# Three orders changed in a two-block transformer kernel: the loads of a norm's rows, the context rows, and the row maxima of a neighbourhood attention

## What is computed

```python
for l in range(2):
    h = layer_norm(a * h + hybrid_mixer(h, ...), ln1_g[l], ln1_b[l])
    h = layer_norm(a * h + cross_attention(h, mem, ...), ln2_g[l], ln2_b[l])
    h = layer_norm(a * h + swiglu(h, ffn_wi[l], ffn_wo[l]), ln3_g[l], ln3_b[l])

sh_a, sc_a, g_a, sh_f, sc_f, g_f = adaln(c, w_ada, b_ada)
hc = rms(ctx) * (1 + csc_a) + csh_a               # the context rows
q, k, v, u, vs = project(rms(h) * (1 + sc_a) + sh_a)
kc, vc = project_kv(hc)
s_win = q @ k_win * scale + bias                  # 8 heads of 64, 256 rows
s = concatenate([s_win, q @ kc * scale])
o_na = softmax(s) @ [v_win, vc]
o_sg = gelu(u) * (w_s @ layernorm(gelu(vs)) + b_s)
x = h + g_a * (concatenate([rms(o_na), rms(o_sg)]) * out_gain) @ w_out
x = x + g_f * hier_moe(rms(x) * (1 + sc_f) + sh_f)
```

## Time and profile before

| | |
|---|---|
| runs | 1566.18, 1569.23, 1570.77 us |
| median | 1569.23 us |
| profiled execution | 1569.23 us |
| its span | 1567.3 us |
| mean granted TensorE clock | 0.993 |
| PE busy | 1536.3 us (98%) |
| DVE busy | 1167.5 us (74%) |
| ACT busy | 920.0 us (59%) |

### The profile page before, as it was taken

How to read it: one execution, slowest core, us unless ns; L and a number is a source line. 1 busy time by engine, 2 the same in 40 slices (tenths; PEclk the granted TensorE clock), 3 DMA queues, 4 the chain that set the end, 5 groups by cost and what they waited for, 6 DMA issues and landing times.

```text
span 1567.3 us, 20279 instructions
## 1 busy us (share of the span) xinstructions
PE 1536.3 (98%) x8024; PEld 1288.4 (82%) x8024; DVE 1167.5 (74%) x1628; ACT 920.0 (59%) x1421; POOL 82.2 (5%) x75
## 2 busy tenths in 40 slices
PE   9999999999999999999999999999999989999997
PEld 9988898888888799889888887888867778878785
DVE  7448866667885683688566679877676789999998
ACT  6468644655444444775447554544355468888884
POOL 0010000001000000100000000000200000000005
PEclk9999999999999999999999999999899999999999
DMA  7535335437775354553354458884441349999994
GB/s 288 208 123 218 135 116 215 161 135 260 256 271 210 134 211 161 188 188 133 137 215 165 158 216 322 335 320 149 165 151 54 113 152 378 365 377 374 369 368 166
DMA packets 52201, 339.35 MB, mean 217 GB/s; under 512 B 7835, under 2 KB 8477, under 8 KB 13316
## 3 DMA queue, kind: packets, MB, share of 16 engines
q1 hardware_dynamic: 48932, 331.79, 56.9%
q0 software_dynamic: 3168, 6.20, 1.1%
HBM read 332.82 MB, written 10.49 MB: 219 GB/s over the span
## 4 chain that ended last, share of the span: by engine, by line
PE 89%; DVE 6%; ACT 2%; issue 1%; DMA 1%; POOL 1%; SPq 0%; DVEq 0%; ACTq 0%; POOLq 0%
PE bank L843 26%; PE bank L845 25%; PE bank L844 25%; PE bank L849 5%; DVE wls L2255 2%; PE bank L1002 2%; PE bank L1130 1%; DMA raw<-in_ws_dram 1%; PE bank L1191 1%; PE bank L1169 1%; PE bank L1110 1%; PE bank L1390 1%; POOL sm L3214 1%; ACT whs L1611 1%; DVE arena L2234 0%
## 5 line engine op out<-in xcount | busy, mean ns | idle before, releaser
L2255 DVE TENSOR_TENSOR wls<-raw,whs 128x1024 fp32r<-128x1024 f32 x426 | 507.0, 1226 | 164.6 <-ACT whs L1611 163.8
L1611 ACT ACTIVATE whs<-raw 128x1024 fp32r<-128x1024 f32 x426 | 429.4, 1052 | 209.9 <-PE bank L845 166.6
L843 PE MATMUL bank<-whs,P1h 128*128 128x512 f32 (+1 forms) x732 | 290.5, 397 | 2.1 <-issue 2.1
L845 PE MATMUL bank<-whs,P1l 128*128 128x512 f32 (+1 forms) x732 | 284.5, 389 | 0.0
L844 PE MATMUL bank<-wls,P1h 128*128 128x512 f32 (+1 forms) x732 | 283.7, 388 | 0.0
L843 PE MATMUL bank<-whs,P0h 128*128 128x512 f32 (+1 forms) x640 | 256.0, 400 | 1.3 <-DVE P0l L2225 1.2
L845 PE MATMUL bank<-whs,P0l 128*128 128x512 f32 (+1 forms) x640 | 248.9, 389 | 0.0
L844 PE MATMUL bank<-wls,P0h 128*128 128x512 f32 (+1 forms) x640 | 248.3, 388 | 0.0
L843 PEld LDWEIGHTS bank<-whs,P1h 128*128 128x128 f32 x732 | 137.6, 188 | 29.4 <-issue 3.0
L845 PEld LDWEIGHTS bank<-whs,P1l 128*128 128x128 f32 x732 | 137.4, 188 | 29.0
L844 PEld LDWEIGHTS bank<-wls,P1h 128*128 128x128 f32 x732 | 137.8, 188 | 26.6
(11 more groups left out here) (300 smaller groups left out, 2511.2 us busy)
## 6 DMA issues: line engine op xcount, KB each, us to landing
raw<-in_ws_dram SPq DMA_DIRECT2D x264, 1024.0 KB, 4.9
landing<-in_ws_dram SPq DMA_DIRECT2D x38, 1024.0 KB, 7.0
lnb<-in_ln_g_dram SPq DMA_DIRECT2D x6, 512.0 KB, 5.8
lnb<-in_ln_b_dram SPq DMA_DIRECT2D x6, 512.0 KB, 7.1
ydram<-arena POOLq DMA_DIRECT2D x4, 512.0 KB, 8.5
mid<-in_bias_dram SPq DMA_DIRECT2D x1, 2048.0 KB, 9.5
h<-in_x_dram SPq DMA_DIRECT2D x2, 512.0 KB, 3.7
lnb<-in_mem_dram SPq DMA_DIRECT2D x1, 1024.0 KB, 13.1
```

The source lines that it names most:

```text
L843: e.matmul(out, x[0], w[0], start=start, stop=False, skip_group_check=skip)
L845: return e.matmul(out, x[1], w[0], start=False, stop=stop, skip_group_check=skip)
L1611: e.activation(hi, src, ACT.Copy, bias=0.0, scale=1.0).then_inc(*high.done(n, f))
L2255: e.tensor_tensor(lo, src, f32(hi), ALU.subtract).then_inc(*low.done(n, f))
```

## The change

Three edits. The number for the rows of the second norm is taken at the end of `cq_w` and no longer in `co_w`, so that two weight units that were issued ahead of these rows now stand behind them. The pauses of the context rows are cut from 12 ticks to 4 on PE, ACT and DVE, so that the squares are ACT's at the first tick of the feed-forward, `ctxeps` and `cn` are DVE's at the second to fourth, and the four parts of `ctx_columns` fall at the `between` ticks of chunks 1 to 4, which were those of chunks 3 to 6. And DVE does the row maximum of item i at step i for each item, which it did for two items at every even step. PE's and ACT's orders in the attention stay.

```diff
@@ PE, cross @@
                 mm.here("cq_end", l)
+                issued["n", l, 2] = W.dma
...
                 def loose():
                     W.loose = True
                     W.feed(2)
-                    issued["n", l, 2] = W.dma
@@ PE, after cross(1) @@
                     mm.here("late")
-                    W.side.append(iter([None] * 12))
+                    W.side.append(iter([None] * 4))
@@ ACT @@
                     def ctx_rows():
-                        for _ in range(8):
-                            yield
                         for t in range(2):
                             ac.wait_ge(landed["ctx"])
                             wait_for(at_all("late"))
@@ DVE @@
                     def ctx_rows():
-                        for _ in range(9):
-                            yield
+                        yield
                         for t in range(2):
                             ve.wait_ge(act, "ctxsq", t)
@@ DVE, attention2 @@
                     if i >= 5:
                         weigh2(i - 5)
-                    if i < n and i % 2 == 0:
+                    if i < n:
                         scores2(i)
-                        scores2(i + 1)
                     for f, *at in beside.get(i, ()):
```

## The result

After the change the kernel takes 1579.25 us (median of 4 runs, 1578.11 to 1580.88), before it 1569.09 (4 runs, 1566.18 to 1570.77). The ratio is 1.0061, with a 95% interval of 1.0047 to 1.0075: slower by 9.6 us by the ratio, 7.4 to 11.8 by its interval. The forecast was 1577.0 us. The profiled execution of the changed kernel took 1578.79 us, 1576.9 of them span, 9.6 more than that of before. In 24 further runs on record the changed kernel has a median of 1577.2 us, and the kernel before has 1569.7 in the 56 runs that the experiments are compared with; so 9.6 us may be somewhat high. Lines of helpers have moved by two in it: DVE's L2253 is L2255 of before.

The account below looks back on a forecast made before the run. PE, with an instruction in it for 98% of the span, was taken as the bound, so only its waits and clock count. The edits' 0 + 2.95 + 4.85 = 7.8 us on 1569.2 gave 1577.0 us, range 1569 to 1582.

Parts of the forecast that it names:

- Edit 1, 0: SP's load queue: two weight units behind the norm's row loads still land in time; cost 0.
- Edit 2, the third quarter, 2.75 us: Layer 1's feed-forward: PE waits 2.75 us for unit 145's low half, held up behind ACT's squares.
- Edit 2, the sixth quarter, 1.0 us: Layer 1's feed-forward: PE waits 0.6 and 0.4 us for unit 146's two low halves.
- the prediction's last line: Wrong if squares start before 893, PE's second pair does not wait, or the clock falls in either stretch.
- rival (c): Clock falls where waits grow; 3 us per 10 us stretch, one or two more giving 1580 to 1583 us; chance 0.12.
- Edit 2, the wait at 948, -0.8 us: Layer 1's feed-forward: less DVE lateness shortens PE's wait for a low part; gain 0.8 us, bounds 0 and 1.9.
- Edit 3, 4.85 us: Attention: PE's score pairs wait for late bank reads, 2.0, 1.0, 0.4, 0.95 us, plus small terms; 4.85 us, bounds 0 and 8.
- The sum: Whole kernel: 0 + 2.95 + 4.85 = 7.8 us slower, 1577.0 us.
- (a): Only one of the two stretches, feed-forward or attention, waits: 1573.3 or 1572.2 us; chance 0.22.
- (b): Not slower: DVE's relief at 948 is the whole effect, 1567.3 us, if squares start before about 892; chance 0.10.
- (d): SP's queue edit shows: a unit late by its whole landing costs 4.9 us, 1582 us with the rest; chance 0.02.

Follow-up runs that it names:

- ctx_single: Kernel before with only the context rows' change, one square ahead of unit 145's splits, the other and all behind it as in ctx_behind; 1571.00 us, ratio 1.0012.
- ctx_triple: Kernel before with only the context rows' change, three squares ahead of unit 145's splits (that of t=0 taken twice); 1576.24 us, ratio 1.0045.
- ctx_behind: Kernel before with the context rows early (7 ticks, not 4), the squares behind ACT's splits of units 145 and 146; 1569.90 us, ratio 0.9999.
- rows_only: Kernel before with only the second norm's row number taken at the end of cq_w; 1570.49 us, ratio 0.9999.
- maxima_only: Kernel before with only DVE's row maximum done one item a step; 1573.91 us, ratio 1.0024.
- read_pair: Kernel before with DVE reading both banks at the even step, the odd item's maximum only at the odd step; 1570.86 us, ratio 1.0012.
- single_both: Kernel before with DVE's maximum one item a step and PE also issuing one item's scores a step; 1580.39 us, ratio 1.0070.
- ctx_only: Kernel before with only the context rows' pauses cut from 12 ticks to 4; 1574.42 us, ratio 1.0035.

## Why the prediction was right, point by point

**Edit 1, 0.** Right: 0.9999.

**Edit 2, the third quarter, 2.75 us.** Right in place, in what PE waits for and in size: 2.64 us of idle time, and the start 2.8 us later than the 1.2 us that this execution had brought along. ctx_single, ctx_triple and ctx_behind show that it is the squares' time, and that it goes when they stand behind the splits.

**Edit 2, the sixth quarter, 1.0 us.** Wrong. PE reaches it at 909.85 and does not wait. In its place stands the low clock, 1.72 us, and this is also why nothing waits: PE itself is late. Unit 146's low halves end at 908.5 and 910.3, where the forecast has them (907.5 and 909.3, with the 1.2 us added). At the full clock PE would have been there at 899.97 + 8.16 = 908.1 and have waited some 0.3 and 0.4 us; this is an estimate. So the clock cost 1.7 us and saved 0.7.

The step that failed is the clock, which the sum puts at nothing; the prediction's last line names its fall in either stretch as a sign of being wrong, and it fell. I had set rival (c) against waits of 1.5 us that kept the clock, and had no row of 2.75 us; the same row now gives 1.43 us with the clock kept, and 2.64 and 3.78 us with it lost. The trace of before had a warning that I passed over: behind the wait of 1.39 us at its last transposition (1213.24) the clock is 0.50 from 1215 to 1220. What the Trainium skill says in TensorE: Matmul & The Clock Gate, that the throttled state is the default and activity releases it, agrees with this. The clock cost no 3 us, as (c) had it for a stretch of 10 us, since it was back before 903.5. Per us (c) had it too cheap: in after's trace matmuls start every 0.43 us at the lower clock and every 0.23 at the full one, so some 3.4 us of it cost 1.7, where the 7 against 10 matmuls of the earlier trace rows give 1.0.

**Edit 2, the wait at 948, -0.8 us.** Against the profiled execution it came out as forecast: 0.18 us at 936.20 and 0.43 at 954.13 in place of 1.51, so -0.9. The reason was wrong in part. I took the wait for one that DVE's load sets in every execution. Up to the attention rows_only (edit 1 apart), maxima_only, read_pair and single_both have the order of the kernel before, and they wait 0, 0, 0.72 and 0 us there. So most executions have less to gain than the one that I read. It was slow in one more place: of the one-column matmuls at L1350, 24 took longer, with a granted clock of 0.90 over 1100 to 1105 in place of 1.00. Before, and in rows_only:

```profile
1102.42 3.85 PE L1350 MATMUL bank<-allone,arena 128*128 128x1 f32 x24
```

```profile
1102.33 2.82 PE L1350 MATMUL bank<-allone,arena 128*128 128x1 f32 x24
```

The stretch from the last L1169 to the first score matmul holds all of edit 2. It is 280.6 us in the profiled execution of before, and 277.7 to 278.5 in the four others with its order. The changed kernel takes 283.5 and ctx_only 283.8, ctx_behind 278.2, ctx_single 279.0 and ctx_triple 284.8. Against the one execution edit 2 costs 2.9 us, as forecast (2.95); against the four 5.0 to 6.1, as by the times (5.5, 3.9 to 7.2). The forecast was right for a reference that was itself 2.5 us slow there.

**Edit 3, 4.85 us.** Right in mechanism and size in the trace: 2.07, 1.01, 0.41, 0.99 us for the forecast's 2.0, 1.0, 0.4, 0.95, and scores 5.0 us longer in all. Only a small term stood elsewhere: the first product with v waits no longer than before (0.69 us at L1390), and 0.29 us came at L1407 (1198.13). DVE's idle time ahead of unit 201's low halves became 2.87 us, as forecast. By the times edit 3 is 3.8 us, with an interval (2.0 to 5.5) that holds 4.85.

**The sum.** 7.8 forecast, 9.6 measured. Between the two profiled executions the 9.6 us are 1.2 ahead of the changed stretch (chance, from layer 0), 2.9 in edit 2's stretch, 5.0 in the scores and 0.5 behind them. By the times edit 2 was put too low, by the clock and by a gain that most executions don't have, and edit 3 a little too high. That the forecast fell within 2 us owes something to errors that cancel: the waits of both stretches were right, the clock was missed, and the closeness of the total is partly luck.

**The rivals.** (a) fell: both stretches wait, and each edit alone is slower than before. (b) fell: the squares start at 895.37, not before 892. (c) came true at the size of 1.7 us, with a chance of 0.12 put on it, and the forecast survived it only because it was short. (d) fell with rows_only.

## What to carry to other kernels

In an in-order queue, side work that waits for something late holds up all behind it, however idle the engine looks: ask when its input is written and what stands behind it, and put it behind the work that others need soon. ACT had 4.6 idle us here, and squares of 2.3 us behind them cost PE 2.6 and the clock 1.7; a few splits further back in the queue the same squares cost nothing. Price a new wait of PE with the clock behind it, and before a wait of today is booked as a gain, look in a second execution whether it recurs.

## What the runs showed of the hardware that I had not expected

The granted clock after a wait. Waits of 1.43 us (ctx_single) and 1.51 us (before, at 948) left it at 1.00. Of two waits of 2.07 us at the same score pair, one left it (after) and one was followed by 0.50 (maxima_only). 2.23 us (read_pair) was followed by 0.68 over 5 us, 2.64 us twice by a loss of 1.7 us, 3.78 us by one of 2.9. From 2.64 to 3.78 us of wait the loss grew by as much as the wait, 1.2 us for 1.1.

But the length of the wait does not decide it. At the first score matmuls, ahead of which no edit of the attention acts, all ten executions wait 1.67 to 1.71 us. In eight the clock stays at 1.00 behind it, and in two, ctx_behind and single_both, it falls to 0.50. ctx_behind:

```profile
1147.00:1150.00 3.00, 3.00 (x9) 2.32 (x8) 2.81 (x8) 0.81 (x2) 0.00 (x0) 0.50 0.98 281
```

And the wait of 1.39 us at the attention's last transposition is followed by 0.55 over 1213 to 1215 before, and by 1.00 over 1222 to 1225 after. What decides between the two is not shown.

A fully busy PE can get the low clock too: around the 48 one-column matmuls in layer 0 it is 0.66 over 560 to 565 in some executions and 0.50 in others, with PE busy 5.00 of 5.00 us in each. The time from the first L1169 to the last, which holds nothing of edits 2 and 3 and of edit 1 only layer 0's part, came out in steps of the same 1.7 us: 566.8 in two executions (before, ctx_only), 568.4 to 568.6 in seven, 570.2 in one (read_pair, 298.9 to 869.1). Much of the spread of some 4 us between runs of one kernel may come from such stretches; that was not tried.
